# DeltaNet block inverses in a two-layer backbone: the second direction's levels run half a level behind the first's on TensorE

## What is computed

```python
m = jnp.where(strict, jnp.einsum('bhncd,bhnsd->bhncs', kb, k) * decay, 0.0)
t_inv = lax.linalg.triangular_solve(eye + m, jnp.broadcast_to(eye, m.shape), left_side=True, lower=True)
u = jnp.einsum('bhncs,bhnse->bhnce', t_inv, v * beta[..., None])
w = jnp.einsum('bhncs,bhnsd->bhncd', t_inv, kb * jnp.exp(gam)[..., None])
def step(s, xs):
    v_new = u_c - jnp.einsum('bhcd,bhde->bhce', w_c, s)
    ...
```

## Time and profile before

| | |
|---|---|
| median of three runs | 2473.12 us |
| the profiled execution | 2464.47 us, of which span 2462.7 us |
| TensorE busy | 2379.8 us, 97% of the span |
| VectorE, ScalarE, GpSimd busy | 1459.8, 950.3 and 136.4 us |
| mean granted TensorE clock | 0.989 of full |
| chain that ended last | 90% TensorE; its DeltaNet lines (L1951) 7% |
| HBM | 306.2 MB read, 125 GB/s over the span |

### The profile page before, as it was taken

One profiled execution on the slowest core, in us unless ns is written; L12 is line 12 of the kernel. 1 busy time (PEld: TensorE's weight loads), 2 busy tenths in 40 slices (PEclk: granted clock), 3 DMA queues, 4 the chain that ended last, 5 costly groups with the idle time before them and its releaser, 6 DMA issues.

```text
span 2462.7 us, 37725 instructions
## 1 busy us (share of the span) xinstructions
PE 2379.8 (97%) x15740; PEld 2015.9 (82%) x15740; DVE 1459.8 (59%) x2273; ACT 950.3 (39%) x1552; POOL 136.4 (6%) x170
## 2 busy tenths in 40 slices
PE   6999999999989999999999999999999988999999
PEld 4888888867878888888888888888887778898999
DVE  6877666346668466587655553333354668667655
ACT  4322223356554422242222232222244764544543
POOL 0000000003034000000000000000000204200000
PEclk8999999999999999999999999999999999999999
DMA  7545443211210143335554432222322220044554
GB/s 295 209 183 192 173 156 116 103 35 52 86 36 3 52 154 137 120 120 205 188 197 169 160 113 89 103 98 91 110 101 83 98 90 3 19 174 174 184 189 171
DMA packets 44664, 309.68 MB, mean 126 GB/s; under 512 B 5072, under 2 KB 6224, under 8 KB 7632
## 3 DMA queue, kind: packets, MB, share of 16 engines
q1 hardware_dynamic: 44208, 306.00, 34.1%
q10 hardware_dynamic: 288, 1.27, 0.2%
HBM read 306.20 MB, written 1.05 MB: 125 GB/s over the span
## 4 chain that ended last, share of the span: by engine, by line
PE 90%; DVE 4%; ACT 3%; issue 2%; DMA 1%; SPq 0%; DVEq 0%; ACTq 0%
PE bank L1571 76%; PE bank L1951 7%; PE bank L1564 2%; PE bank L1864 1%; PE bank L1887 1%; DVE u_lo L2256 1%; DMA first_panels<-in_wts 1%; DVE w_lo L2208 1%; PE bank L1583 1%; ACT w_hi L999 1%; PE bank L1873 1%; PE bank L1805 1%; DVE sq L2248 0%; PE bank L1664 0%; PE bank L1595 0%
## 5 line engine op out<-in xcount | busy, mean ns | idle before, releaser
L2208 DVE TENSOR_TENSOR w_lo<-ring,w_hi 128x1024 fp32r<-128x1024 f32 x420 | 510.6, 1224 | 665.6 <-ACT w_hi L999 660.7
L1571 PE MATMUL bank<-u_hi,w_hi 128*128 128x512 f32 (+1 forms) x2272 | 813.5, 358 | 20.8 <-DVE u_lo L2256 12.1
L1571 PE MATMUL bank<-u_hi,w_lo 128*128 128x512 f32 (+1 forms) x2272 | 802.2, 353 | 0.0
L1571 PE MATMUL bank<-u_lo,w_hi 128*128 128x512 f32 (+1 forms) x2272 | 802.0, 353 | 0.0
L999 ACT ACTIVATE w_hi<-ring 128x1024 fp32r<-128x1024 f32 x420 | 443.3, 1059 | 817.7 <-PE bank L1571 802.8
L1571 PEld LDWEIGHTS bank<-u_hi,w_hi 128*128 128x128 f32 x2272 | 430.2, 189 | 89.7 <-issue 16.1
L1571 PEld LDWEIGHTS bank<-u_lo,w_hi 128*128 128x128 f32 x2272 | 430.2, 189 | 59.2
L1571 PEld LDWEIGHTS bank<-u_hi,w_lo 128*128 128x128 f32 x2272 | 430.5, 189 | 57.3
L1571 PE MATMUL bank<-hidden_hi,w_hi 128*128 128x512 f32 (+1 forms) x722 | 258.1, 357 | 0.0
L1571 PE MATMUL bank<-hidden_hi,w_lo 128*128 128x512 f32 (+1 forms) x722 | 257.4, 356 | 0.0
L1571 PE MATMUL bank<-hidden_lo,w_hi 128*128 128x512 f32 (+1 forms) x722 | 257.3, 356 | 0.0
(11 more groups left out here) (257 smaller groups left out, 2465.0 us busy)
## 6 DMA issues: line engine op xcount, KB each, us to landing
ring<-in_wts SPq DMA_DIRECT2D x280, 1024.0 KB, 4.8
first_panels<-in_wts SPq DMA_DIRECT2D x8, 1024.0 KB, 5.7
h<-in_x SPq DMA_DIRECT2D x8, 256.0 KB, 4.7
par<-in_par ACTq DMA_DIRECT2D x2, 620.0 KB, 3.8
out<-h SPq DMA_DIRECT2D x8, 128.0 KB, 3.5
cst<-in_cst SPq DMA_DIRECT2D x1, 724.0 KB, 6.9
mod_par<-in_mod SPq DMA_DIRECT2D x1, 96.0 KB, 5.5
cond<-in_c SPq DMA_DIRECT2D x1, 8.0 KB, 1.9
```

Of the source, the lines that this page charges most:

```text
L1571: last = weights.used(pe.matmul(out, lhs[a], rhs[b], start=start and n == 0, stop=stop and n == 2))
L2208: tt(w_lo[:, b % HALVES, :], half_source(n % RING, part), w_hi[:, b % HALVES, :].bitcast(F32), ALU.subtract).then_inc(panel_left[n % RING] ...
```

## The change

TensorE's order inside the level loop changes; no instruction is added or removed, no wait or semaphore count is changed, and the other engines' streams stay as they are. Before, a level is F of direction 0, F of direction 1, beside 0, S of direction 0, S of direction 1, beside 1. After, S of direction 1 is issued behind the next level's beginning: S(n - 1, 1), F(n, 0), beside(n, 0), S(n, 0), F(n, 1), beside(n, 1), and S of direction 1 of the last level stands behind the loop. `state(1, j - 1)` in level 1 is moved with it, behind F(1, 0) and beside(1, 0).

```diff
                         for d in range(2):
                             if n == 1 and j:
                                 state(d, j - 1)
+                            if d:
+                                second_half(n, 0)
+                            elif n > 1:
+                                second_half(n - 1, 1)
                             first_half(n, d)
-                        beside_level(n, 0)
-                        for d in range(2):
-                            second_half(n, d)
-                        beside_level(n, 1)
+                            beside_level(n, d)
+                    second_half(LEVELS - 1, 1)
                     for d in range(2):
                         pe.wait_ge(beside_ready[d], it + 1)
                         pe.wait_ge(x_ready[d], (it + 1) * LEVELS)
```

## The result

The changed kernel takes 2482.8 us (median of six runs, 2479.43 to 2487.86) against 2472.41 us for the kernel before, measured beside it: 1.0047 times as long, 95% interval 1.0032 to 1.0063. On a second occasion (the first experiment) the ratio was 1.0077, interval 1.0065 to 1.0089. Slower, as forecast: by 10.4 us on the first occasion and 17.6 on the second, where the sum of the prediction has 17.7. The forecast of 2490.8 us is 8 us above the first median and 6 us above the second. The profiled execution took 2487.86 us.

What follows compares the result with a forecast made beforehand. It took TensorE's groups of small products nearly to bound the DeltaNet levels. Bare levels 7.7 + 2.2, odd pairs 3.2, level 5 3.5, level 1 -0.8 and ScalarE 1.9 gave +17.7 on 2473.12, so 2490.8 us; range +11 to +27.

Steps and rivals of the forecast that it cites:

- the sign given: Sign that the prediction is right: each DeltaNet stage some 8 to 10 us longer, all else equal.
- ScalarE's delay: Level 5 of three turns with `keep_scores`: ScalarE's level 4 work holds back the copy of Y, +0.6 us each, 1.9 in all.
- A bare level: Level with nothing beside: TensorE waits for Y's copy twice, 3.50 us; +0.96, or +0.73 against the slower 2.77.
- S is 0.57 more: In a level with nothing beside, each S adds 0.57 us after the 1.18 from F to S.
- The pairs of odd levels 3 and 4: Odd turns, level 3 with `keyed` plus bare level 4: 7.11 us before, 7.9 after, +0.8 in each of 4 pairs.
- Levels with beside work: Levels with work beside: F and that work last 1.60 us, hiding the copy; the level stays 4.33 us, nothing gained or lost.
- the filled wait: Level 1 of three odd turns: `outs` of direction 0 lies in the wait for VectorE's preparation, -0.4 us each.
- Turn 2 of layer 1, level 1, "0": Layer 1's turn 2, level 1: 0 us change, as TensorE has no wait there to fill.
- The +0.6 in layer 2's turn 2: Level 1 of layer 2's turn 2: +0.6 us, where no wait stands ahead of F1.
- Level 4 of turns 2, +0.73 each: Bare level 4 where VectorE's `scores` went before: +0.73 us against the slower 2.77 us level.
- Level 5: Last level of each turn: +0.25 us in six turns with `decay` beside, +1.0 in two with nothing beside; 3.5 in all.
- This rival: Clock stays at its lower level through five bare levels of both first turns: 8.6 us more, 2499.5 us; chance 10%.

Runs made afterwards that it cites:

- the first experiment: The changed kernel run again without any edit, against the kernel before; 2484.51 us against 2466.92, ratio 1.0077.
- e9: Changed kernel with VectorE's level 1 adding direction 0's output ahead of direction 1's update; 2485.88 us, ratio 1.0067 against the kernel before.
- e5: The kernel before, unedited, measured once more against itself; ratio 0.9999.
- e8: Changed kernel with sixteen unread small products behind each F in bare levels 2 to 4; 2486.86 us, ratio 1.007 against the kernel before.
- e7: Changed kernel with ScalarE's copy of Y cut into four pieces, one per head; ratio 1.0123 against the kernel before.
- e4: Changed kernel reordered so the other direction's product stands between F and S of one direction; 2493.2 us, ratio 1.0106 against the kernel before.

## Why the prediction was right, and where its steps were off

The mechanism stood as written: the run S, F is unbroken and the wait for Y's copy is open twice a bare level. The size of the sum did not come out of its terms alone: they miss by up to 2.1 us in both directions, and the sum is close because the misses partly cancel, which is luck. The stages are 7.2 and 8.0 us longer; 8 to 10 each was the sign given. The steps, in groups of turns and levels (predicted: the terms of the sum; measured: differences between the two first traces' updates of direction 1; us):

| where | predicted | measured |
|---|---|---|
| layer 1, turn 0, levels 1 to 4 | +1.6 | +2.5 |
| layer 2, turn 0, levels 1 to 4 | +2.8 | +4.1 |
| odd turns, levels 1 and 2 | +2.6 | +0.5 |
| odd turns, levels 3 and 4 | +3.2 | +1.9 |
| turns 2, levels 1 and 2 | +0.6 | +2.7 |
| turns 2, levels 3 and 4 | +1.5 | +0.1 |
| level 5, with ScalarE's delay | +5.4 | +3.5 |
| sum | +17.7 | +15.2 |

- *A bare level: 3.50 predicted, 3.27 measured.* F to S is right to the hundredth: the copy starts 0.75 after F, S loads 0.43 to 0.44 after the copy. What was mis-sized is the step "S is 0.57 more". 0.57 us is how long a group of 16 loads takes by itself; back to back, two take 1.01, so the second starts 0.44 or 0.45 us after the first. That stood in the earlier trace rows (the row of 32 loads at 712.36) and I read past it. Two groups a level, 0.12 each: 0.23 us a bare level. A half level is then 1.18 + 0.45 = 1.63. The pairs of odd levels 3 and 4 cost 0.49 and not 0.8, in the main for the same reason.
- *What bounds a bare level before.* The prediction calls the levels "nearly bound by TensorE's own groups", with 0.21 us of waiting. At 0.45 us a group the four need 1.8 of the 2.54 us. What the level is near is one direction's ring, 1.18 + 1.27 = 2.45 us by the prediction's own pieces. Two copies of the kernel before (layer 2, turn 0) show it:

```profile
2044.71 0.38 ACT L1409 ACTIVATE work<-bank 128x256 f32<-128x256 f32 x1 [0.21 <-PE bank L1951]
2045.50 0.38 ACT L1409 ACTIVATE work<-bank 128x256 f32<-128x256 f32 x1 [0.40 <-PE bank L1951]
```

  F1 stands 0.79 us behind F0 and not 0.45. The row of 64 loads at 2044.75 begins 0.75 us ahead of the second copy, so it begins with F1, and its 0.21 us are a wait for direction 1's update, not direction 0's. The price of the change was not touched by this, as 2.54 us was measured; what is free in a bare level was.
- *Levels with beside work stay at 4.33:* right (turn 2 of layer 1, level 3: updates of direction 1 at 11.71 and 16.04 us from the turn's start).
- *Level 1 and 2 of odd turns:* the filled wait gave 0.8 us and not 0.4; with 0.73 for bare level 2 nothing is lost in three turns, and 0.7 in layer 2's turn 1, which has no such outputs.
- *Turn 2 of layer 1, level 1, "0":* here a step failed outright. I asked what stands behind each moved S on TensorE, and not which of VectorE's instructions stand behind the later update of direction 1 and hold a bank. A wait of 1.31 us, of which e9 gave 1.2 back. The +0.6 in layer 2's turn 2 was +0.9. Nor do all the 21 bare levels have nothing between F0 and S0: in level 1 of layer 2's turns 1 and 2 `state(1, j - 1)` stands there.
- *Level 4 of turns 2, +0.73 each:* nearly nothing (+0.04). Before, `keyed(1)` and VectorE's row make that level 3.80 us long, not the 2.77 of turn 0 from which I took the price.
- *ScalarE's delay:* +0.7 in turn 0 of layer 1, and +0.16 in both turns 2, where I had 0.6 three times (1.8 in sum, not the 1.9 of the prediction). *Level 5:* +0.13 with `decay` (0.25 predicted), +0.81 bare (1.0 predicted).
- *The clock.* This rival came true in part beside the forecast. Layer 2, turn 0 of the changed kernel, copies of Y and the window:

```profile
2046.64 0.38 ACT L1409 ACTIVATE work<-bank 128x256 f32<-128x256 f32 x1 [2.62 <-PE bank L1951]
...
2047.07 1.78 PEld L1951 LDWEIGHTS bank<-work 64*64 64x64 f32 x32 [0.66 <-ACT work L1409]
...
2049.09 0.38 ACT L1409 ACTIVATE work<-bank 128x256 f32<-128x256 f32 x1 [2.07 <-PE bank L1951]
```

```profile
2043.70:2053.90 10.20, 8.10 (x128) 7.24 (x128) 6.14 (x13) 1.47 (x5) 5.66 (x7) 0.50 0.01 2
2053.90:2068.00 14.10, 11.84 (x262) 10.79 (x261) 9.40 (x27) 7.47 (x21) 2.70 (x5) 1.00 0.01 2
2127.00:2149.00 22.00, 18.77 (x407) 17.16 (x406) 15.88 (x43) 4.97 (x13) 9.95 (x12) 1.00 0.01 3
```

At 1.2 GHz a half level is 2.45 us and not 1.63, so 1.64 a level; the price of the rival, 1.7, was right. It was paid over about one and a quarter levels in each first turn, some 2.0 us in layer 2 and 1 to 2 in layer 1 (estimates: measured differences less what the levels cost at the full clock), and not over five. It filled the gap that the mis-sized group left open: part of the good sum is luck. Before, the clock is at the lower level in layer 1's turn 0 too, to 707.8 us, and in layer 2's as well (to 2039.0 us, and to 2037.1 in e5), so part of this, in layer 2 above all, is only where the low stretch fell. In layer 1 the change does keep the clock low longer, by the fourteen traces told under e8. That the waits in bare levels are the reason is only argued: where they were filled (e8) nothing changed that could be seen. The Trainium skill ("TensorE: Matmul & The Clock Gate", section "A second HAM failure mode: psum-queue depth-cycling") warns of short idles between groups. Ten waits of up to 0.62 us in the last two turns did not bring the clock down (granted 1.00 throughout both; the last window above is the last turn); in e7, with waits of 0.81 us, and in e4, with one of 2.44 us ahead, it was at the lower level for 34 and 17 us. In layer 2 no run here separates the rule from chance; layer 1's first turn goes its way, without showing which idles do it.
- *What moved outside the turns.* I wrote that the prediction would be wrong if stages outside moved. They did, by up to 15 us, but between executions of like kernels as well (2265 and 2261 for the same kernel before), so this says nothing of the change. About 7 us of it are the two paces of the last stretch, which one and the same kernel shows; the remainder, in which stretches vary from trace to trace, is not explained, and no experiment here was made for it.

## What to carry to other kernels

When two dependent rings share an in-order engine, write down for every hand-over what stands between the producer and its consumer in that engine's stream; an order that makes "one's second half and the other's first half" adjacent also makes some other pair adjacent, and here that was the one with the longer latency. The order that alternates the rings at each step (F0 F1 S0 S1) runs within 0.1 us of one ring's own length (2.54 against 2.45 us), and beside work is worth something only where a wait stands. Take the pitch of back-to-back groups from a row that holds two of them, not from the length of one; and for each instruction that is delayed, list what is queued behind it on the other engines and which banks that holds.

## What the runs showed of the hardware that was not expected

- One ScalarE copy of 128x256 out of a bank takes 0.38 us; four of 128x64 take 0.57 us together, not four times a fixed cost.
- Sixteen records of small fp32 products (0.55 us of loads) fit into an idle of 0.62 us and leave the half level at 1.63 us, as e8's rows show.
- The part of the kernel that no experiment touched on TensorE took from 2261 to 2276 us in fourteen profiled executions: more than the change itself costs. In its last stretch TensorE, busy throughout at a granted clock of 1.00, took either 1191 or 1237 matmul records in 140 us, in two executions of one kernel.
- In layer 1's first turn the granted clock was 0.50 for 10.2 us in all six traces of orders half a level apart throughout, and for 6.8 us in all eight others.
- In e7 the granted clock stayed at 0.50 for 34.1 us while TensorE's loads and products kept it busy for 28.97 of them; in e4 it was 0.50 with TensorE busy for 16.37 of 16.50 us.
